# Order of work around the paired down projections of four feed-forward stages in a two-block transformer kernel

## The reference

```python
def swiglu(h, w_gu, w_down):
    gate, up = jnp.split(h @ w_gu, 2, axis=-1)
    return (jax.nn.silu(gate) * up) @ w_down

def sublayer(x, shift, scale, gate, g_pre, g_post, fn, res_weight):
    h = rmsnorm(x, g_pre) * (1 + scale[:, None, :]) + shift[:, None, :]
    return x + res_weight * gate[:, None, :] * rmsnorm(fn(h), g_post)

mods = jnp.split(c_act @ cond_w[layer] + cond_b[layer], 3 * N_SUBLAYERS, axis=-1)
cos, sin = rope_tables(positions)
```

## Time and profile before

| quantity | value |
|---|---|
| median of 3 runs | 2756.17 us |
| the profiled execution, its own time | 2749.45 us |
| its span in the profile | 2747.7 us |
| PE busy | 2435.2 us (89%) |
| DVE busy | 1781.6 us (65%) |
| PE idle until weight sums (L932 behind L2304), four stages | 12.7 + 3.0 us |
| gate and up units of the ffn stages | 48 to 186, 427 to 565, 685 to 823, 1001 to 1139 us |

### The profile page before, as it was taken

One profiled execution on the slowest core, in us unless ns is written; L12 is line 12 of the kernel. 1 busy time (PEld: TensorE's weight loads), 2 busy tenths in 40 slices (PEclk: granted clock), 3 DMA queues, 4 the chain that ended last, 5 costly groups with the idle time before them and its releaser, 6 DMA issues. The chain is left out here.

```text
span 2747.7 us, 26964 instructions
## 1 busy us (share of the span) xinstructions
PE 2435.2 (89%) x9731; PEld 1554.6 (57%) x9731; DVE 1781.6 (65%) x3934; ACT 620.7 (23%) x1778; POOL 694.2 (25%) x698
## 2 busy tenths in 40 slices
PE   7999999999999999999998977878879778877776
PEld 6874558857884678668654533634436544432222
DVE  4677145665566545743798875687886878874454
ACT  2001210001000210000233333342333523332222
POOL 1110001100110001100244444344444443443432
PEclk9999999999999999999999999989999989999999
DMA  9985426964894349866799999999999999999997
GB/s 382 377 355 202 153 98 267 361 243 158 330 365 163 143 185 381 355 240 241 316 416 420 421 421 422 421 405 422 418 420 396 421 421 421 413 407 422 421 422 317
DMA packets 120525, 931.61 MB, mean 339 GB/s; under 512 B 15134, under 2 KB 16566, under 8 KB 20423
## 3 DMA queue, kind: packets, MB, share of 16 engines
q0 software_dynamic: 94032, 670.65, 59.7%
q1 hardware_dynamic: 26358, 259.23, 23.8%
HBM read 928.74 MB, written 1.09 MB: 338 GB/s over the span
## 5 line engine op out<-in xcount | busy, mean ns | idle before, releaser
L1376 PE MATMUL psF<-ring,p_diag 128*128 128x512 f32 x1792 | 874.2, 633 | 236.0 <-ACT p_diag L1822 235.9
L715 POOL DMA_INDIRECT ring<-in_peer_uv_dram,lamt x512 | 601.6, 1175 | 958.8 <-PE psF L1376 746.5
L2690 DVE SCALAR_TENSOR_TENSOR ring<-ring,h 128x1024 f32<-128x1024 f32 x512 | 620.8, 1224 | 341.6 <-DMA ring<-in_peer_uv_dram,lamt 338.2
L1376 PEld LDWEIGHTS psF<-ring,p_diag 128*128 128x128 f32 x1792 | 340.9, 200 | 699.2 <-ACT p_diag L1822 354.0
L1026 PE MATMUL psR<-hT,ring 128*128 128x256 f32 x2560 | 553.2, 379 | 0.0
L1026 PEld LDWEIGHTS psR<-hT,ring 128*128 128x128 f32 x2560 | 486.1, 190 | 65.9
L1813 ACT ACTIVATE small<-small 128x2 f32<-128x2 f32 x255 | 51.8, 203 | 807.1 <-DVE ring L2690 806.8
L543 POOL DMA_DIRECT2D mring<-in_mod_t_dram x80 | 42.7, 533 | 731.4 <-DVE mring L2086 727.4
L2261 DVE TENSOR_TENSOR arena<-arena,psR 128x256 f32<-128x256 f32 x80 | 33.7, 421 | 205.9 <-ACT arena L1683 205.7
L1683 ACT ACTIVATE arena<-psR 128x256 f32<-128x256 f32 x86 | 33.0, 384 | 568.0 <-PE psR L1026 521.8
L1822 ACT ACTIVATE p_diag<-ident,small 128x128 f32<-128x128 f32 x446 | 158.2, 395 | 8.3
(11 more groups left out here) (373 smaller groups left out, 2731.7 us busy)
## 6 DMA issues: line engine op xcount, KB each, us to landing
ring<-in_gu_t_dram SPq DMA_DIRECT2D x44, 2048.0 KB, 10.4
mring<-in_mod_t_dram POOLq DMA_DIRECT2D x80, 1024.0 KB, 8.0
M<-in_mod_t_dram POOLq DMA_DIRECT2D x40, 1024.0 KB, 8.2
ring<-in_down_t_dram SPq DMA_DIRECT2D x20, 2048.0 KB, 9.4
mring<-in_tail_w_dram SPq DMA_DIRECT2D x40, 1024.0 KB, 9.2
ring<-in_conv_in_t_dram SPq DMA_DIRECT2D x12, 2048.0 KB, 8.9
ring<-in_gla_in_t_dram SPq DMA_DIRECT2D x6, 2048.0 KB, 7.7
ring<-in_out_t_dram SPq DMA_DIRECT2D x6, 2048.0 KB, 7.8
```

The lines of the kernel that those rows point to most:

```text
L715: pool.indirect_dma_start(out=pair(n % PAIRS), out_offset=None, in_=rows, in_offset=bass.IndirectOffsetOnAxis(ap=s_idx[:, c:c + 1], axis=0 ...
L1376: ins = pe.matmul(psF[:, b, f * HALF:(f + 1) * HALF], p_diag[:, n % PAIRS, :], row_v(n % PAIRS)[:, f * HALF:(f + 1) * HALF], start=(i == 0 ...
L2690: dve.scalar_tensor_tensor(row_u(c), row_u(c), 1.0, h[:, b, :], ALU.mult, ALU.mult, accum_out=p_dots[:, c:c + 1]).then_inc(dot_done, 1)
```

## The change

Four edits. (1) In the pairs 0 to 8 PE takes the products that read the weight sums (6, 7, 4) first and signals `weights_sums_used` after three products, where it was after five. (2) `halves_done` spreads all half steps of a stage evenly over the 20 units from tile 2 to tile 21, and none is left for the down phase. (3) `sum_weights(1)` moves ahead of the last `sum_acts`. (4) `tables()` moves to tile 11 of stage 0; its two last operations, which need ScalarE's exponential, become `lambda_tables()` behind `sum_weights(3)`.

```diff
     def halves_done(st, unit):
-        return min(2 * len(BESIDE[st.n]), max(unit - 1, 0) * 4 // 3)
+        return min(2 * len(BESIDE[st.n]), max(unit - 1, 0) * 2 * len(BESIDE[st.n]) // 20)
...
             for p in range(PAIRED - 2):
                 sums_ready(p)
-                for m in (1, 6, 7, 5):
+                for m in (6, 7, 4):
                     ins = product(m, p)
-                if p == 6:
+                ins.then_inc(weights_sums_used, 1)
+                for m in (1, 5) if p in LATE_PAIRS else (1, 5, 2, 3):
+                    ins = product(m, p)
+                if p in (1, 3, 6):
                     ins.then_inc(w_used, 1)
-                product(4, p).then_inc(weights_sums_used, 1)
-                if p not in LATE_PAIRS:
-                    for m in (2, 3):
-                        ins = product(m, p)
-                    if p in (1, 3):
-                        ins.then_inc(w_used, 1)
...
                 for _ in range(halves_done(st, j) - halves_done(st, j - 1)):
                     half_step()
+                if st.n == 0 and j == FT // 2:
+                    tables()
                 if j == FT - 2:
                     sum_weights(st, 0)
+            sum_weights(st, 1)
             dve.wait_ge(unit_stored, u)
             sum_acts(st, PAIRED - 1)
-            sum_weights(st, 1)
-            if st.n == 0:
-                tables()
             for p in range(2, PAIRED):
                 sum_weights(st, p)
-                if halves_taken.n < sum(2 * len(BESIDE[n]) for n in BESIDE if n <= st.n):
-                    half_step()
+                if st.n == 0 and p == 3:
+                    lambda_tables()
             sum_products(st)
```

More of the change, by code:

```diff
@@ L2902, in tables, with lambda_tables @@
             dve.tensor_reduce(lam2, lp, AX, ALU.add).then_inc(act_input_ready, 1)
+        def lambda_tables():
             from_act(2)
```

## The result

The change makes the kernel slower: 2770.94 us, the median of 6 runs (2768.36 to 2775.30), against 2756.07 for the kernel before in 6 runs beside them (2752.46 to 2757.42). The ratio is 1.0055, with a 95% interval of 1.0043 to 1.0067, so about 12 to 18 us. That lies above the predicted 2757.0 us and outside its range of 2751 to 2763, and "same" had been given 81%.

A forecast was written before the change was run, and what follows sets the result against it. PE was taken as the bound, busy 89%, with 15.7 us of waits for weight sums to win. Stages 0, 2, 4 and 6 gave -0.7 - 0.1 - 0.3 + 1.9 = +0.8 us on the median 2756.17: 2757.0 us, range 2751 to 2763.

The forecast's parts named there:

- PE's waits in the ffn stages: PE's waits for weight sums in the four ffn stages, 15.7 us in 14 waits, as all the change can win.
- The counts of instructions: DVE's operations ahead of the weight sums, counted per stage: -0.7, -0.1, -0.3 and +1.9 us, together +0.8 us.
- Edit 1's 1.7 us a stage: At pair 10 of each ffn stage, earlier release of DVE shortens PE's wait: 1.7 us each, 6.9 us in all.
- The stages 2 and 4: Extra half step before pair 1 costs 1.6 and 1.4 us, less 1.7 at pair 10: -0.1 and -0.3 us.
- The tail moved as a block: The tail's own work was forecast to stay untouched and move as a block.
- The transfers: Stage 0's gate and up phase: six more modulation transfers, 406 GB/s needed by its end, taken to cost 0.
- my own signs of being wrong: Total under 8 us, DVE waits for `mring` or `M` above 3 us, or PE idle inside gate and up.
- the bound of +24 us a stage: Stages 0 and 6, if POOL's queue kept 206 GB/s: 33.6 MB would take 163 us, +24 us each.
- The half steps come late: Rival, stages 0 and 6: POOL's queue falls behind, delaying PE through `sum_weights(0)`; 4 us a stage, +8, 2765 us; 11%.
- The clock: Slow clock stretches behind PE's waits: bounds -1.7 to +10 us, taken as 0; rival of two or three more, 2760.4 us, 12%.

## Why the prediction was wrong

**What held.** The reading that PE's waits in the ffn stages are what counts: 14.6 us more of them, a median 14.9 us later. That these agree to 0.3 us is partly luck, since the profiled executions differ by 22.9 us (see "What the base was"). The counts of instructions: with the transfers in time, pair 0 of stage 0 waits 3.26 us, where I had 3.3. Edit 1's 1.7 us a stage, at the three other stages too. The order of the places where DVE is late: pairs 0 and 1. The stages 2 and 4: from the start of gate and up to pair 10 they came out at 0.3 us less each, where I had 0.1 and 0.3. The tail moved as a block: from its first instruction to the end it takes 1454.6 us before and 1454.4 after.

**The step that failed** is the one under "The transfers": "I take 0, as 406 is nearer to 384 than to anything not seen". It compared mean rates: 406 GB/s needed, 384 moved, 419 seen in the best 35 us. The rate did come out near the need, at 402 GB/s. What the step put at nothing without a reason is that transfers land later when the engines are nearly full, and that with three buffers this slows the half steps. The DMA engines were busy at a share of 0.92 to 0.97 in the last 103 us of the phase before, and of 0.97 to 0.99 after; I had even quoted the share of 1.01 beside the 419. A modulation transfer then landed in 9.9 or 11.8 us instead of 8.9 or 9.0. With three buffers that gives one every 4.2 to 4.8 us, and one was wanted every 4.3. DVE waited 71.1 us for these transfers, which was one of my own signs of being wrong (above 3 us). The two experiments with half the bytes show that this is the cause: with either queue's bytes halved the loss of 15 us is gone, while every instruction of the change is still there. That the three buffers are a part of it follows from the count only, since no run had another number of them.

**Its size.** Stage 0 came out 7.5 us later instead of 0.7 earlier, stage 6 13.2 later instead of 1.9. Over the count that is 8.2 and 11.3 us, a third and a half of the bound of +24 us a stage. POOL's queue did not stay at its 206 GB/s: it moved 31.07 MB in 139 us, 224 GB/s.

**The rival "The half steps come late"** was the right mechanism, with the passing on to PE as described; only the last wait stood one tile earlier, ahead of the product of tile 20. It had 11%, and its price of 4 us a stage was too small. I took a shortfall of 3% in rate. The shortfall against the wanted pace was 4.63 to 4.3 us, 8%. Of the 33.0 us that DVE waited for transfers in stage 0 only some 7 reached PE; the rest went into the idle time that DVE had before and into PE's lead of two units. As an argument against it I had put that the wait of 1.13 us came behind start-up loads. In truth the change then brought the whole phase close to that state: the shares of 0.97 to 0.99 above are near the 1.01 of that stretch.

**The clock.** I had taken 0 of a range of -1.7 to +10. The old slow stretch at 1190 is gone. New ones, behind the waits of 10.60 and 10.11 us and the 2.25 of stage 6, make PE's work 2.4, 1.9 and 1.7 us longer. The first two are followed by a wait at pair 1 that would otherwise have been longer by as much, so only the third adds to the time, as much as the old one gives back. The net of 0 came out, but by luck: the waits behind it are not the ones that I had counted. The waits of 2.47 and 2.09 us in stages 2 and 4 were followed by no slow stretch. In the table by stretch, after:

```profile
190.00:200.00 10.00, 3.42 (x4) 1.51 (x5) 9.00 (x20) 0.00 (x0) 1.05 (x2) 0.56 0.98 412
...
290.00:300.00 10.00, 10.00 (x16) 3.72 (x15) 1.20 (x2) 9.32 (x11) 0.00 (x0) 0.66 0.43 180
```

0.56 is near the 1.2 GHz level. The second row is in a stage that the change doesn't touch and that took 3.2 us longer than before. Together with 1.9 us more around 920 it makes 5 us in which the two profiled executions differ by chance, or by a cause that I don't know. The kernel before had such a stretch at 280 (granted clock 0.83).

**What the base was.** The profiled execution of before, 2749.45 us, is among its quickest; its median is 6.6 higher. The two profiled tails are equally long, so these executions differ in the first 1300 us. It may be the clock, but there is one profile of before only, and so this stays open. It also blurs the comparison of the profiles (23 us apart) with that of the medians (15).

**Not tried:** a fourth buffer for half steps. By the count above it would relax the pace that three allow, but not the share of the DMA engines. Such a run would tell how much of the loss is the number of buffers.

## What to carry to other kernels

Before work with transfers is put into a phase, read the DMA engines' busy share of just this phase, stretch by stretch, and not only the GB/s. In stage 0, at 0.92 and above, the mean rate still rose (from 384 to 402 GB/s), but transfers landed later. Then compare how often a transfer is wanted with what its landing time and the number of buffers allow: stage 2 had shares of 0.91 and 0.98 and no wait, as it wanted a transfer every 4.9 us, and stage 0 had late ones, as it wanted one every 4.3. Work that waits for a transfer does not belong directly ahead of the instruction that the bottleneck engine waits for: putting the weight sums ahead of the half steps at tiles 20 and 21 was worth 14 us in the change, and 4 where the transfers were in time. And several edits that seem to be one idea are to be timed one by one: here three brought 20 us, and the fourth hid them.

## What the runs showed of the hardware

- The 16 DMA engines were busy at nearly the same share at quite different rates: in stage 0 after, 0.97 at 375 GB/s and 0.99 at 408; in stage 0 before, 0.97 at 376. In the first 35 us of after it was 1.01 at 426. A rate alone does not tell whether they are full.
- Two queues on nearly full engines slow each other: in stage 0 modulation transfers of 1 MB landed in 9.9 and 11.8 us (median) in the change, and in 8.3 and 7.9 us once the gate and up transfers of the other queue had half the bytes.
- Fillers kept TensorE's granted clock at 1.00 through a gap of 10 us (four matmul instructions in 1.95 us behind them), and a wait of 5.05 us that began 7 us after the last filler dropped it all the same (3.75 us).
- A wait of about 2 us is sometimes followed by a slow stretch and sometimes not, at the same place: behind 2.09 us at pair 1 of stage 4 the four instructions took 1.96 us in the change, and 3.35 us in the run with the new spread in stages 2 and 4 only.
